# Layer 1's second feed-forward: five gate/up pairs on the unnormalised x, the other seventeen on the normalised x in two passes per product

## The reference

```python
def rms_norm(x): return x * rsqrt(mean(x * x, axis=-1) + EPS)
def modulate(h, shift, scale): return h * (1.0 + scale) + shift
def swiglu(h, w1, w3, w2): return (silu(h @ w1) * (h @ w3)) @ w2

x = x + mx[5] * (mix_x @ w_out[l])                      # "out1"
x = x + 0.5 * mx[8] * swiglu(modulate(rms_norm(x), mx[6], mx[7]),
                             ffn2_w1[l], ffn2_w3[l], ffn2_w2[l])   # "ffn2"
```

## Time and profile before

| | |
|---|---|
| median of three runs | 2370.79 us (2369.74 to 2370.86) |
| profiled execution | 2369.99 us, span 2368.2 us |
| TensorE (PE) busy | 2348.6 us, 99% of the span |
| weight loads (PEld) | 2039.4 us, 86%, beside PE |
| VectorE (DVE) | 1534.2 us, 65% |
| ScalarE (ACT) | 1017.9 us, 43% |
| GpSimd (POOL) | 405.8 us, 17% |
| chain that ended last | 95% on PE |
| DMA | 360.76 MB, mean 152 GB/s |

### The profile page before, as it was taken

One profiled execution on the slowest core, in us unless ns is written; L12 is line 12 of the kernel. 1 busy time (PEld: TensorE's weight loads), 2 busy tenths in 40 slices (PEclk: granted clock), 3 DMA queues, 4 the chain that ended last, 5 costly groups with the idle time before them and its releaser, 6 DMA issues.

```text
span 2368.2 us, 36508 instructions
## 1 busy us (share of the span) xinstructions
PE 2348.6 (99%) x14378; PEld 2039.4 (86%) x14378; DVE 1534.2 (65%) x2611; ACT 1017.9 (43%) x1734; POOL 405.8 (17%) x427
## 2 busy tenths in 40 slices
PE   9999999999999999999999999999999999999998
PEld 6888889777888888988888877999989999999887
DVE  5888775784698865523322576766677665667874
ACT  5222234654522223422223465545456444456663
POOL 2221221240122131111011121121000220000110
PEclk9999999999999999999999999999999999999999
DMA  9565542212366755222222222555534555434553
GB/s 355 195 209 206 182 159 89 66 55 98 114 212 238 247 207 178 89 98 98 98 94 95 81 99 82 173 184 187 172 118 142 173 175 176 156 120 162 190 188 134
DMA packets 97865, 360.76 MB, mean 152 GB/s; under 512 B 11024, under 2 KB 11792, under 8 KB 96544
## 3 DMA queue, kind: packets, MB, share of 16 engines
q1 hardware_dynamic: 75744, 272.84, 34.3%
q0 software_dynamic: 21952, 85.59, 10.1%
HBM read 357.34 MB, written 1.05 MB: 151 GB/s over the span
## 4 chain that ended last, share of the span: by engine, by line
PE 95%; DVE 1%; ACT 1%; issue 1%; DMA 1%; POOL 0%; DVEq 0%; ACTq 0%; POOLq 0%
PE bank L816 26%; PE bank L818 26%; PE bank L817 26%; PE bank L823 6%; PE bank L824 3%; PE bank L1170 1%; PE bank L1140 1%; PE bank L1158 1%; PE bank L1192 1%; DMA arena<-w_mod_first_dram 1%; PE bank L1119 0%; PE bank L1079 0%; ACT ring_high L1390 0%; PE bank L1344 0%; PE bank L1334 0%
## 5 line engine op out<-in xcount | busy, mean ns | idle before, releaser
L1920 DVE TENSOR_TENSOR ring_low<-ring,ring_high 128x1024 fp32r<-128x1024 f32 x520 | 641.1, 1233 | 484.4 <-ACT ring_high L1390 482.4
L816 PE MATMUL bank<-x_parts,ring_high 128*128 128x512 f32 (+2 forms) x2308 | 799.2, 346 | 2.3 <-POOL x_parts L637 1.4
L1390 ACT ACTIVATE ring_high<-ring 128x1024 fp32r<-128x1024 f32 x520 | 547.9, 1054 | 572.8 <-PE bank L818 528.8
L818 PE MATMUL bank<-x_parts,ring_low 128*128 128x512 f32 (+2 forms) x2308 | 786.3, 341 | 0.0
L817 PE MATMUL bank<-x_parts,ring_high 128*128 128x512 f32 (+2 forms) x2308 | 784.9, 340 | 0.0
L816 PEld LDWEIGHTS bank<-x_parts,ring_high 128*128 128x128 f32 x2308 | 434.6, 188 | 68.0 <-issue 13.2
L818 PEld LDWEIGHTS bank<-x_parts,ring_low 128*128 128x128 f32 x2308 | 434.6, 188 | 47.5
L817 PEld LDWEIGHTS bank<-x_parts,ring_high 128*128 128x128 f32 x2308 | 435.1, 189 | 46.9 <-issue 1.0
L647 POOL TENSOR_TENSOR hidden_parts<-fresh,hidden_parts 128x512 fp32r<-128x512 f32 (+2 forms) x132 | 203.4, 1541 | 1006.2 <-ACT hidden_parts L1523 1006.2
L1933 DVE CUSTOM_DVE_ANT_0 mod_products<-mod_ring,csilu 128x1024 bf16<-128x1024 f32 x224 | 303.1, 1388 | 30.3 <-DMA mod_ring<-w_mod_dram 28.7
L816 PE MATMUL bank<-hidden_parts,ring_high 128*128 128x512 f32 (+2 forms) x814 | 280.9, 345 | 0.2 <-POOL hidden_parts L647 0.2
(11 more groups left out here) (268 smaller groups left out, 2756.8 us busy)
## 6 DMA issues: line engine op xcount, KB each, us to landing
ring<-stream_dram SPq DMA_DIRECT2D x517, 512.0 KB, 3.4
mod_ring<-w_mod_dram POOLq DMA_DIRECT2D x128, 512.0 KB, 4.4
arena<-w_mod_first_dram POOLq DMA_DIRECT2D x8, 1024.0 KB, 11.7
ring<-stream_dram POOLq DMA_DIRECT2D x3, 512.0 KB, 10.8
arena<-na_bias_dram POOLq DMA_DIRECT2D x2, 768.0 KB, 11.8
mod_ring<-consts_dram POOLq DMA_DIRECT2D x1, 1076.0 KB, 5.3
resid<-x_dram POOLq DMA_DIRECT2D x2, 512.0 KB, 6.0
resid<-ctx_dram POOLq DMA_DIRECT2D x2, 512.0 KB, 7.2
```

The costliest lines, as they stand in the source:

```text
L816: pe.matmul(out, w[0][:, b], xh, start=start, stop=False)
L818: return pe.matmul(out, w[1][:, b], xh, start=False, stop=stop)
L1390: act.activation(high[:, i % SPLIT], ring[:, u % LOADED], ACT.Copy).then_inc(high_parts, 1)
L1920: dve.tensor_tensor(low[:, u % LOADED], ring[:, u % LOADED], high_f[:, i % SPLIT], ALU.subtract).then_inc(low_parts, 1)
```

## The change

The first five pairs stay as they are: 258 columns, three passes, scaled afterwards. From pair 5 on (`EARLY_PAIRS = 5`, so 17 pairs, 34 units) TensorE multiplies the properly normalised and modulated x with `wide_product`. Those parts are made during the first pairs, chunk by chunk, in two groups of four (`LATER`): GpSimd multiplies the residual by `row_scale` (`later_scaled`), ScalarE applies gain and shift twice, once into the high part and once in place (`later_high`), and the low part is the difference, made by VectorE for even chunks (`later_even`) and by GpSimd for odd ones (`later_odd`). They go to `x_parts`, which the mixing step no longer needs by then. From pair 5 on VectorE's two scaling products per pair and the copies of the shift's share are gone; ScalarE's `half_out` and VectorE's `halves_added` come in, twice per pair.

```diff
+EARLY_PAIRS = 5
+LATER = [range(0, 4), range(4, 8)]
...
+        def wide_units(tag, f=0):
+
+            return tag == ("ffn", 1) or tag == ("ffn2", 1) and f >= EARLY_PAIRS
+
+        def later_parts():
+
+            hi, lo = x_parts(N1)
+            place = xf[:, 0:2 * KC * N1].rearrange("p (k c n) -> p k c n", k=2, c=KC)[:, 0, :, NX:N1]
+            return hi[:, :, 0:NX], lo[:, :, 0:NX], place
...
+            def later_scaled(chunks):
+
+                _, _, place = later_parts()
+                for c in chunks:
+                    pool.tensor_tensor(place[:, c], resid[:, c, META:META + NX], row_scale[:, 0:NX], ALU.mult).then_inc(
+                        *made("x_low_pool", ("ffn2", 1), c, "scaled"))
+
+            def later_odd(chunks):
+
+                hi, lo, place = later_parts()
+                for c in chunks:
+                    if c % 2:
+                        pool.wait_ge(*when("shifted", ("ffn2", 1), c, "later"))
+                        pool.tensor_tensor(lo[:, c], place[:, c], hi[:, c].bitcast(F32), ALU.subtract).then_inc(
+                            *made("x_low_pool", ("ffn2", 1), c, "later"))
+                        ev.table[("x_low", ("ffn2", 1), c, "later")] = ev.table[("x_low_pool", ("ffn2", 1), c, "later")]
...
+                        if tag == ("ffn2", 1) and f < len(LATER):
+                            if f == 0:
+                                pool.wait_ge(*when("rstd", (("out1", 1), 0)))
+                            later_scaled(LATER[f])
+                        if tag == ("ffn2", 1) and 2 <= f < 2 + len(LATER):
+                            later_odd(LATER[f - 2])
...
+                        if tag == ("ffn2", 1) and f == EARLY_PAIRS:
+                            xh, xl, _ = later_parts()
+                            for c in range(KC):
+                                pe.wait_ge(*when("x_low", ("ffn2", 1), c, "later"))
+                            cols = NX
                         for what in ("gate", "up")[h == 0 and f == 1 and begun(prev) > 2:]:
                             p = take(what, tag, h, f)
                             w = weights()
                             for c in range(KC):
-                                if wide_units(tag):
+                                if wide_units(tag, f):
...
+            def later_high(f):
+
+                hi, _, place = later_parts()
+                for c in LATER[f - 1]:
+                    shift = mod[:, 1, 0, 6 * KC + c:6 * KC + c + 1]
+                    gain = mod[:, 1, 0, 7 * KC + c:7 * KC + c + 1]
+                    act.wait_ge(*when("x_low_pool", ("ffn2", 1), c, "scaled"))
+                    act.activation(hi[:, c], place[:, c], ACT.Identity, bias=shift, scale=gain).then_inc(
+                        *made("x_high", ("ffn2", 1), c, "later"))
+                    act.activation(place[:, c], place[:, c], ACT.Identity, bias=shift, scale=gain).then_inc(
+                        *made("shifted", ("ffn2", 1), c, "later"))
...
+                            if tag == ("ffn2", 1) and 1 <= f <= len(LATER):
+                                later_high(f)
+                            if wide_units(tag, f):
                                 half_out(tag, "gate", f)
                                 split_ahead(1)
-                            if tag in SCALED_LATE:
+                            if tag == ("ffn2", 1) and wide_units(tag, f):
+                                act.wait_ge(*when("halves_added", tag, "gate", f))
+                                act.wait_ge(*when("hidden", tag, h, f - 2))
+                                act.activation(act_out[:, f % 2, 0:n], squares[:, f % 2, 0:NX], ACT.Silu).then_inc(
+                                    *made("silu", tag, h, f))
+                            elif tag in SCALED_LATE:
...
+            def later_even(f):
+
+                hi, lo, place = later_parts()
+                for c in LATER[f - 1]:
+                    if c % 2 == 0:
+                        dve.wait_ge(*when("shifted", ("ffn2", 1), c, "later"))
+                        dve.tensor_tensor(lo[:, c], place[:, c], hi[:, c].bitcast(F32), ALU.subtract).then_inc(
+                            *made("x_low_dve", ("ffn2", 1), c, "later"))
+                        ev.table[("x_low", ("ffn2", 1), c, "later")] = ev.table[("x_low_dve", ("ffn2", 1), c, "later")]
...
+                    if tag == ("ffn2", 1) and wide_units(tag, g):
+                        x = halves_added(tag, "up", g, p)
+                        dve.wait_ge(*when("silu", tag, h, g))
+                        dve.tensor_tensor(fresh[:, g % 2, 0:n], x, act_out[:, g % 2, 0:n], ALU.mult).then_inc(
+                            *made("hidden", tag, h, g))
+                    elif late:
...
+                    if tag == ("ffn2", 1) and 1 <= g <= len(LATER):
+                        later_even(g)
```

More of the change, by code:

```diff
@@ L1481, in half_out @@
                 act.wait_ge(*when(what, tag, 0, f))
-                if f >= 2:
-                    act.wait_ge(*when("halves_added", what, f - 2))
+                if wide_units(tag, f - 2) and f >= 2:
+                    act.wait_ge(*when("halves_added", tag, what, f - 2))
                 at = 0 if what == "gate" else NX
                 act.activation(squares[:, f % 2, at:at + NX], bank(what, tag, 0, f)[:, NX:2 * NX], ACT.Copy).then_inc(
-                    *made("half_out", what, f))
+                    *made("half_out", tag, what, f))
+            def later_high(f):
[8 more added lines that the diff above has]
+                        *made("shifted", ("ffn2", 1), c, "later"))
             def ffn(tag, n, parts):
@@ L1518, in ffn @@
                                     act.activation(csilu[:, s], csilu[:, s], ACT.Silu).then_inc(*made("c_silu", l, s))
-                            if (tag != ("ffn1", 0) or h or f) and not wide_units(tag):
+                            if (tag != ("ffn1", 0) or h or f) and not wide_units(tag, f):
                                 split_ahead(1)
@@ L2004, in halves_added @@
                 x = squares[:, f % 2, at:at + NX]
[L2005 removed]
+                dve.wait_ge(*when("half_out", tag, what, f))
                 dve.tensor_tensor(x, p[:, 0:NX], x, ALU.add).then_inc(
[L2007 to L2009 removed]
+                    *made("halves_added", tag, what, f, frees=(what, tag, 0, f)))
+                dve.wait_ge(*when("halves_added", tag, what, f))
+                return x
+            def later_even(f):
[6 more added lines that the diff above has]
+                        ev.table[("x_low", ("ffn2", 1), c, "later")] = ev.table[("x_low_dve", ("ffn2", 1), c, "later")]
             def ffn(tag, n, parts, l=None, before=None):
@@ L2015, in ffn @@
                     h, g = f // nf, f % nf
-                    if late:
+                    if late and g == 0:
+                        dve.wait_ge(*when("rstd", (before, 0)))
+                    if tag == ("ffn2", 1) and wide_units(tag, g):
+                        dve.wait_ge(*when("gate", tag, h, g))
+                        halves_added(tag, "gate", g, bank("gate", tag, h, g))
+                    elif late:
                         dve.wait_ge(*when("gate", tag, h, g))
                         p = bank("gate", tag, h, g)
-                        if g == 0:
-                            dve.wait_ge(*when("rstd", (before, 0)))
                         if tag == ("ffn2", 1):
```

11 lines of the change are left out of this document (3 added, 8 removed).

## The result

| | before | changed |
|---|---|---|
| median of 11 runs each | 2369.94 us | 2375.54 us |
| lowest and highest | 2369.42, 2370.86 | 2373.77, 2378.31 |
| ratio of the times | | 1.0023, 95% interval [1.0015, 1.0031] |
| profiled execution, span | 2369.99, 2368.2 us | 2376.99, 2375.2 us |

The forecast was +2.8 us and 2373.6 us. The median of 2375.54 us lies 0.1 us above the top of its range (2370.2 to 2375.4). The run times also spread over 4.5 us, where those of the kernel before spread over 1.4 us.

A forecast was written before the change was run, and what follows sets the result against it. TensorE, busy 99% of the span, was taken to bound the kernel. A 3.0 us gain, 4.4 us of waits and 1.4 us of lower clock summed to +2.8 us: 2373.6 us, range 2370.2 to 2375.4 us.

The forecast's parts named there:

- the last line: End of the prediction: the forecast as a whole is wrong if the time is below 2370 or above 2375.5 us.
- the sum: Total of gain, waits and clock: -3.0 + 4.4 + 1.4 = +2.8 us, giving a median of 2373.6 us.
- A first wait of 1.2 us: TensorE ahead of unit 8: the unit is ready at 1526.9, wanted at 1525.73, behind ScalarE's later split.
- 4.4 us late in all: TensorE starting unit 10 at 1535.9 instead of 1531.50: 1.2 us ahead of unit 8, 3.2 ahead of unit 10.
- the walk: Step-by-step timing of the added GpSimd, ScalarE and VectorE work in program order, from the norm's root at 1506.7 to unit 10.
- not all of it: GpSimd beside VectorE's split: the trace was said to show only part of the shared-port blocking; 0.73 us lost.
- Rival C: GpSimd's low-part chain blocked for the whole overlap, 2.0 us an operation: TensorE waits 6.8 us, +5.2 us, 2376.0; 8%.
- The clock: 1.4 us forecast: TensorE's clock falls at the 3.2 us blank ahead of unit 10; 1.4 us taken, between nothing and 2.6 us.
- The gain of 3.0 us: 34 units of 8 products from pair 5 on go from 0.3615 to 0.3504 us a product: 272 x 0.0111.

The follow-up runs named there:

- e1: Changed kernel with GpSimd scaling all eight chunks at once, ahead of the hidden layer's first low part; 2372.74 us, ratio 1.0014.
- e8: Changed kernel with only the odd low parts one hidden chunk earlier in GpSimd's program, scaling still in two groups; 2371.72 us, ratio 1.0006.
- e2: Changed kernel with all eight chunks scaled at once and the odd low parts one hidden chunk earlier; 2368.66 us, ratio 0.9996.
- e3: Changed kernel with 24 extra 258-column matmuls, results overwritten, where TensorE waits ahead of unit 10; 2374.90 us, ratio 1.0019.
- e4: Changed kernel with all preparation and its wait, but units 10 to 43 still multiplied in three passes of 258 columns; 2378.46 us (four runs), ratio 1.0035.
- e9: The kernel of e2 unchanged, profiled once more for the pitch; 2369.19 us, against 2371.18 us for e2's profiled execution.
- e10: Changed kernel with six pairs ahead, scaling at once, activations spread, plus one overwritten 64-column matmul before each two-pass gate and up unit; 2372.79 us, ratio 1.0012.

## Why the prediction was right or wrong, point by point

**Right.** Where TensorE waits, how often, who releases it (VectorE's split ahead of unit 8, GpSimd's last odd low part ahead of unit 10), and that the clock falls. That nothing starves after pair 5. e1 and e8 show each wait to hang on its own place in GpSimd's order, e2 that both shrink, to 0.5 and 0.7 us, when only the order changes.

**Not right: how far.** The forecast gave 90% to a change within 0.2% and 9% to more; the median moved by 0.23%. At 2375.54 us it is also just past the 2375.5 that the last line names as the sign of a wrong forecast. The mechanism held; the terms of the sum were too small, and in the profiled execution all of them erred the same way.

**"A first wait of 1.2 us" and "4.4 us late in all": 2.1 and 5.8 us.** Two prices of the walk were too low. ScalarE's activation with gain and shift was priced at 0.40 us by the row of L1449, which has a gain only the earlier trace rows; with both it takes 0.49, 0.7 us for eight and 0.2 us for chunk 7's two at the end of the second group. That is the whole 0.9 us of the first wait: GpSimd's second four scalings took 4.17 us where the walk had 4.1. And GpSimd and VectorE hold each other up both ways. I took from the earlier trace rows that GpSimd is slowed beside a split, and let VectorE pass untouched. Its 1.06 and 1.75 us at 1528.70 show that it is not; they stand on the way to the second wait and add 1.1 us. So the low part of hidden chunk 2 ends 2.1 us later than in the walk. The last two odd low parts then take 1.58 us instead of 2.42, as no split meets them, and TensorE starts 0.35 us behind the last instead of 0.1: together 1.4 us more than forecast. This is read from the timelines; no run takes VectorE's share out by itself.

**The rule that I weighed and priced wrong.** I wrote that the trace shows the loss of the shared port "but not all of it". It does show all of it. GpSimd's operation at 1517.27 met a split that ended at 1518.12 and itself ended at 1518.73, 0.61 us after the earlier trace rows. That is its 0.73 us alone less 0.12 us; that these 0.12 us lie at its start and do not need the port is an inference. VectorE's scaling from 1518.11 on has a bank for one input and doesn't hold it up. The Trainium skill ("SBUF — State Buffer", Terms) has the rule as it is: an exclusive lock for the full instruction, and the loser is blocked. What I missed is that the loser can be VectorE too: by these durations the lock works for whoever is first. A row of GpSimd operations back to back, which the kernel before has nowhere in this stage, is first again and again. Rival C named the mechanism and gave it 8%, at a price of +5.2 us; the mechanism was there, on VectorE's side, but only as a part of the 5.8 us. That C's 2376.0 us is nearer to the measured time than the forecast's is luck: its own sign, GpSimd operations of 1.9 us or more, did not come, the longest in this stage being 1.71 us.

**The clock: 1.4 us forecast, 1.6 us in the profile.** A blank of 2.0 us went ahead of the fall in e3 and e8, shorter than the one I had reckoned with. In the five profiles with a wait of 2.0 us or more (the changed kernel, e1, e3, e4, e8) it fell each time, though in the changed kernel and in e4 not at the first; in the profiles whose waits stay under 1.5 us it fell only at the kernel's end. What decides whether a blank of 2.0 us is followed by a fall is open. A run of the changed kernel has two chances to fall and, as e4's 6.8 us show, can stay low for longer. That is the upper part of its spread, argued from the other profiles and not seen in one of its own.

**The gain of 3.0 us.** It came from the pitch of ("ffn", 1), 0.3504 us with its mean-square product in it. In this stage the pitch is one of two others. From unit 10 on, where no mean-square product lies, three passes took 0.3602 us a product before (1531.50 to 1629.12 over 271 distances), so with 0.3467 the gain is 272 x 0.0135 = 3.7 us, with 0.3533 it is 1.9 us, and then the down product, which I had left out as unchanged, loses 154 x 0.0066 = 1.0 us too. So the terms are, in a faster run, 5.8 + 1.6 - 3.7 = +3.7 us and in a slower one 5.8 + 1.6 - 1.9 + 1.0 = +6.5 us, 2373.6 and 2376.4 with before at 2369.9. The measured times begin at 2373.77 and have their median between the two, at 2375.54; the ones above 2376.4, up to 2378.31, would want a longer or a second fall. The sum for the profiled execution is 0.5 (ahead of the stage) + 6.5 = 7.0 us, which is what its span is longer by.

What decides which rhythm a row falls into is open. The fall of the clock does not (e1 and e3 have the fast one after a fall, e2 the slow one without), nor does the order of the programs (e2 and e9 are one kernel). e10 narrows it: a small disturbance ahead of a unit is enough to change it within one execution.

## What to carry to other kernels

Work that other engines do "beside" TensorE has to be followed in program order through every engine it touches, with what is queued behind it; here moving eight small GpSimd instructions (e2), without one more or less, let unit 10 start 1.9 us late instead of 5.8 and kept the clock up. A new blank on TensorE has a second price beside its length: here each profile with one of 2.0 us or more had a stretch of low clock that cost 1.6 us or more, half of what the change was forecast to bring. And when the times of a kernel stand in groups, take several profiles of it before a term is read from one.

## What the runs showed of the hardware

- A row of wide products (512 and 256 columns in turn) ran at 0.3467 or at 0.3533 us a product, constant through one run's 426 products, either value from run to run of the same kernel. With one small matmul ahead of each unit (e10) both values stood in one execution.
- One extra matmul of 64 columns in front of a unit of eight cost 0.11 us in e10's trace, and 0.16 us by the medians, in which the slower rhythm is counted too.
- GpSimd's 128x256 two-input operations and VectorE's two-input ones on SBUF excluded each other, by their durations in the changed kernel: a split 1.22 us alone took 1.75 us behind GpSimd, a product 0.48 us alone 1.07 us; GpSimd's 0.73 us became the rest of the split plus 0.60 us.
- ScalarE's 128x256 activation started its successor 0.49 us later with gain and shift from columns, 0.40 us with a gain alone.
- A blank of 2.0 us on TensorE was followed by 3.4 us at 1.2 GHz in e3 and e8, and by none in the changed kernel and in e4; the blank of 3.0 to 3.1 us by 3.4 us in the changed kernel and e1 and by 6.8 us in e4.
